# Hybrid decoder step: steps of a packed triangular inverse moved from among the matmul products to places beside the key scores and value products

## The reference

```python
proj = x @ w_in                       # 2048 x 7184
# group A: gated DeltaNet, 8 heads x 128: conv width 4, silu, l2 norms,
#   chunked delta rule over chunks of 128 rows for the prompt:
#   (I + strictly lower part of beta * k k^T * decay)^-1 applied to v and k
# group B: MoBA attention, 8 heads x 128: the prompt's own block;
#   samples score all 2048 cached keys, keep the best 3 blocks of 256,
#   softmax over them and their own key, times the cached values
out = concat(oa, ob) @ w_out;  x = layer_norm(ALPHA * x + out)
x = layer_norm(ALPHA * x + cross_attention(x, 256 memory tokens))
x = layer_norm(ALPHA * x + swiglu(x, w1, w2))   # hidden 5632
```

## Time and profile before

| what | value |
|---|---|
| device time, median of 3 | 1552.3 us (1551.79 to 1552.63) |
| the profiled execution | 1559.02 us |
| its span, first to last instruction | 1557.2 us |
| mean granted TensorE clock | 0.992 |
| busy: PE, DVE, ACT, POOL | 97%, 59%, 42%, 6% |
| DMA moved | 365.11 MB, mean 234 GB/s |
| chain that ended last | PE 79%, DVE 7%, ACT 4%, DMA 4% |

### The profile page before, as it was taken

How to read it: one execution, slowest core, us unless ns; L and a number is a source line. 1 busy time by engine, 2 the same in 40 slices (tenths; PEclk the granted TensorE clock), 3 DMA queues, 4 the chain that set the end, 5 groups by cost and what they waited for, 6 DMA issues and landing times.

```text
span 1557.2 us, 36665 instructions
## 1 busy us (share of the span) xinstructions
PE 1508.7 (97%) x15464; PEld 1458.0 (94%) x15464; DVE 912.4 (59%) x1217; ACT 651.1 (42%) x771; POOL 89.0 (6%) x126
## 2 busy tenths in 40 slices
PE   7999999999889999999999999999999999999996
PEld 7899899999778999997999999999999999999995
DVE  4445646458643466664786666666666644455566
ACT  5344344434425454463643334443333333333344
POOL 0000000002233100001000000000000000000000
PEclk9999999999999999999999999999999999999998
DMA  8788989896678876656555555556767655555453
GB/s 290 262 340 331 338 307 363 304 340 250 248 261 300 311 272 242 217 179 254 190 177 174 171 179 188 169 183 229 251 233 257 208 174 185 189 169 181 162 183 116
DMA packets 72527, 365.11 MB, mean 234 GB/s; under 512 B 9072, under 2 KB 10424, under 8 KB 45656
## 3 DMA queue, kind: packets, MB, share of 16 engines
q1 hardware_dynamic: 56960, 310.00, 56.1%
q0 software_dynamic: 13664, 52.31, 9.1%
q10 hardware_dynamic: 1792, 1.20, 0.3%
HBM read 353.20 MB, written 10.47 MB: 234 GB/s over the span
## 4 chain that ended last, share of the span: by engine, by line
PE 79%; DVE 7%; ACT 4%; DMA 4%; SPq 3%; issue 2%; another core or an unknown queue 1%; POOL 0%; ACTq 0%; DVEq 0%
PE psum_g L538 22%; PE psum_g L539 22%; PE psum_g L540 22%; PE M L2220 3%; DVE wl L522 2%; ACT wh L517 2%; SPq L659 2%; PE M L538 1%; PE M L539 1%; PE M L540 1%; PE psum_g L2560 1%; DMA raw<-w_in_t 1%; DMA sraw<-cache_k_t 1%; PE M L2235 1%
## 5 line engine op out<-in xcount | busy, mean ns | idle before, releaser
L538 PE MATMUL psum_g<-xh,wh 128*128 128x264 f32 (+1 forms) x2382 | 696.5, 292 | 5.9 <-DVE wl L522 3.8
L539 PE MATMUL psum_g<-xl,wh 128*128 128x264 f32 (+1 forms) x2382 | 676.8, 284 | 0.0
L540 PE MATMUL psum_g<-xh,wl 128*128 128x264 f32 (+1 forms) x2382 | 675.9, 284 | 0.0
L522 DVE TENSOR_TENSOR wl<-raw,wh 128x2048 fp32r<-128x2048 f32 (+1 forms) x205 | 461.6, 2252 | 302.4 <-ACT wh L517 301.9
L517 ACT CAST wh<-raw 128x2048 fp32r<-128x2048 f32 (+1 forms) x221 | 414.4, 1875 | 248.2 <-PE psum_g L540 194.4
L538 PEld LDWEIGHTS psum_g<-xh,wh 128*128 128x128 f32 x2382 | 449.4, 189 | 21.7 <-issue 13.3
L539 PEld LDWEIGHTS psum_g<-xl,wh 128*128 128x128 f32 x2382 | 449.8, 189 | 3.2 <-issue 2.9
L540 PEld LDWEIGHTS psum_g<-xh,wl 128*128 128x128 f32 x2382 | 447.9, 188 | 0.0
L538 PE MATMUL psum_g<-gh,wh 128*128 128x264 f32 x704 | 200.3, 285 | 0.2 <-DVE wl L522 0.2
L539 PE MATMUL psum_g<-gl,wh 128*128 128x264 f32 x704 | 199.4, 283 | 0.0
L540 PE MATMUL psum_g<-gh,wl 128*128 128x264 f32 x704 | 199.4, 283 | 0.0
(11 more groups left out here) (474 smaller groups left out, 1693.5 us busy)
## 6 DMA issues: line engine op xcount, KB each, us to landing
raw<-w_t SPq DMA_DIRECT2D x88, 1024.0 KB
raw<-w_in_t SPq DMA_DIRECT2D x53, 1024.0 KB
kring<-cache_k_t SPq DMA_DIRECT2D x96, 512.0 KB, 5.5
sraw<-cache_k_t SPq DMA_DIRECT2D x32, 512.0 KB, 6.5
raw<-w_out_t SPq DMA_DIRECT2D x16, 1024.0 KB
raw<-w2a_t SPq DMA_DIRECT2D x16, 1024.0 KB
raw<-w2b_t SPq DMA_DIRECT2D x16, 1024.0 KB
raw<-w2c_t SPq DMA_DIRECT2D x16, 768.0 KB
```

Source lines behind the costliest of these rows:

```text
L522: eng.tensor_tensor(wl[:, u % 2, 0:nk], raw[:, u % 2, 0:nk], wh[:, u % 2, 0:nk].bitcast(F32), ALU.subtract).then_inc(raw_used, 1)
L538: nc.tensor.matmul(out, hi_w, x_hi(k), start=(k == order[0]), stop=False)
L539: nc.tensor.matmul(out, hi_w, x_lo(k), start=False, stop=False)
L540: last = nc.tensor.matmul(out, lo_w, x_hi(k), start=False, stop=(k == order[-1]))
```

## The change

A table `steps_at(u, place)` says which steps stand at which place. In pairs 0 to 2 steps 7 to 18 stand three a unit at place 3, that is in `behind`: the first ahead of the burst, the second between its halves, the third behind it. In pair 3 they stand two at a time around a group of value products, at place 1 (k = 7) or place 3. Step 19 moves from unit r = 4 to place 0 of r = 5, and `first_chunk` on ScalarE with it. VectorE does all the steps of a place where the place stands in its order; `head_out` comes ahead of `step(1)`. The signal of step 14 on VectorE is split, so that TensorE's step 15 waits for the first of two quarters only.

```diff
-                      [n for l in lv[1:-1] for n in (f"t1_{l}", f"x_{l}", f"y_{l + 1}")] +
+                      [n for l in lv[1:-1] for n in (f"t1_{l}", f"x_{l}") + (("xq",) if l == SMALL - 1 else ()) + (f"y_{l + 1}",)] +
...
+        def steps_at(u, place):
+            p, r = pair_at(u)
+            if p < 0 or r in (0, 7):
+                return (4 * r + place,) if p >= 0 else ()
+            if r == 1 and place < 2:
+                return (4 + place,)
+            if r > 4:
+                return (4 * r + place if (r, place) != (5, 0) else 19,)
+            if p < 3:
+                return tuple(range(3 * r + 4, 3 * r + 7)) if place == 3 else ()
+            if place == 3:
+                return {1: (7, 8), 2: (11, 12), 3: (15, 16)}.get(r, ())
+            return {2: (9, 10), 3: (13, 14), 4: (17, 18)}.get(r, ()) if place == 1 else ()
...
                 elif r == 5:
+                    first_chunk(p)
                     first_state(p)
...
-                if r == 4:
-                    first_chunk(p)
-                elif r == 5:
+                if r == 5:
                     second_chunk(p)
...
                         for q in range(2):
-                            ins = nc.vector.tensor_tensor(quarter(xlo, q), xc[part(q)], small(B_, part(q)), ALU.subtract)
-                        vec(ins)
-                        wait(dve, b_dve, f"x_{l}", p)
+                            vec(nc.vector.tensor_tensor(quarter(xlo, q), xc[part(q)], small(B_, part(q)), ALU.subtract))
+                        wait(dve, b_dve, "xq", p)
...
-                step(1)
                 if 0 <= j - 1 < H:
                     head_out(j - 1)
+                step(1)
...
-            def score(i, u):
+            def score(i, u, heads=range(H)):
...
+            def tiles_at(u, place):
+                steps = steps_at(u, place)
+                return steps if steps and 7 <= steps[0] <= 18 else ()
...
-                if k % 4 == 3 and 0 <= r < 7:
-                    delta(p, 4 * r + k // 4)
+                if k % 4 == 3 and not tiles_at(u, k // 4):
+                    for s in steps_at(u, k // 4):
+                        delta(p, s)
...
+                    first, *rest = tiles_at(u, 1) or (None,)
+                    if first:
+                        delta(p, first)
                     for group in groups_at(u, 0):
                         page_values(group)
+                    for s in rest:
+                        delta(p, s)
...
+                first, *rest = tiles_at(u, 3) or (None,)
+                if first:
+                    delta(p, first)
                 for j in bursts_at(u):
-                    score(j // 4, j % 4)
+                    for half in range(2):
+                        score(j // 4, j % 4, range(4 * half, 4 * half + 4))
+                        if rest:
+                            delta(p, rest.pop(0))
                 if u in (UNITS - 5, UNITS - 4):
                     state_rows(u - (UNITS - 5))
                 for group in groups_at(u, 1):
                     page_values(group)
+                for s in rest:
+                    delta(p, s)
```

More of the change, by code:

```diff
@@ L1724, in _, with step @@
                 j = u - FIRST_HEAD
-                step = lambda c: delta(p, 4 * r + c) if p >= 0 else None
+                def step(place):
+                    for s in steps_at(u, place):
+                        delta(p, s)
                 if 0 <= j - 1 < H:
@@ L2216, in score @@
                     pe.wait_ge(k_full[m % K_RING], 16 * (m // K_RING + 1))
-                for h in range(H):
+                for h in heads:
                     for p, m in enumerate(pages):
```

## The result

| what | before | after |
|---|---|---|
| device time, median | 1553.5 us (1551.79 to 1558.8, 11 runs) | 1571.37 us (1561.01 to 1580.3, 11 runs) |
| the profiled execution | 1559.02 us | 1570.05 us |
| stretches of clock 0.50 in it | 4 | 7 |

The ratio is 1.0106 (95% interval 1.0083 to 1.0128): slower by 1.1%, some 16 us by the ratio and 17.9 by the two medians. The median lies above the range of 1550.5 to 1569.

The account below looks back on a forecast made before the run. TensorE, busy 97% of the span, was taken as the bound, so time between its product groups counts. 1.65 - 0.8 + 3.2 = +4.05 us on the profiled execution, carried over unscaled to 1556.4 us; range 1550.5 to 1569.

Parts of the forecast that it names:

- +1.65 us for pairs 0 to 2: Pairs 0 to 2: each ends 0.55 us late, the stand in unit 14 outweighing savings elsewhere; +1.65 us for three.
- the clock's +3.2 us: TensorE's clock: new stands bring two more falls to half clock than now, +3.2 us; bounds 0 and +9.6.
- -0.8 us for pair 3: Pair 3, beside the value products: six steps leave the products, signals get through, the pair gains 0.8 us.
- The edges: TensorE, half burst to packed step: the change of shape takes 0.21 us; bounds 0.03 and 0.21.
- The cheap change of shape: Faster rival: half burst to packed step takes 0.03 us instead of 0.21; -3.4 us, 1548.9 us; chance 0.14.
- The stand in unit 14: TensorE ahead of step 14, also units 22 and 30: waits 2.5 us for VectorE, busy with convolution and normalising.
- 1.8 us a pair: Pairs 0 to 2: steps placed around bursts save 1.3 us a pair, 1.8 us with the waits.
- head's values 0.35 us late: Pair 3: head turn 1.7 us later because two answers precede the maximum, but the head's values only 0.35 us late.
- The held signals: Slower rival, pair 3: step signals held until 0.8 us after the last gather; +16 us, 1568.8 us; chance 0.26.
- Little happens: Rival: the 0.21 us edge holds but the clock stays up in the stands; +0.9 us, 1553.2 us; chance 0.18.
- three times -0.65 us: Pairs 0 to 2 at the low bound of the change of shape: each pair gains 0.65 us instead of losing.

Follow-up runs that it names:

- two free repeats: The changed kernel, unedited, twice more on one chip, no pair 3 step held: 1566.62 and 1568.19 us, beside 1554.46 for the kernel before.
- x9: Kernel before with new places in pair 3 only, gathers waiting for the step's signal and the scores' maximum ahead of the answers: ratio 0.9951 to the kernel before.
- x14: Changed kernel, with pair 3's gathers waiting for the step's signal and the maximum ahead of the answers: ratio 0.9979 to the kernel before.
- x8: Kernel before with new places in pair 3 only, its gathers waiting for the step's signal: ratio 0.9998 to the kernel before.
- x7: Changed kernel, with pair 3's gathers also waiting for the signal of the step behind the value products: ratio 1.0040 to the kernel before.
- x1: Changed kernel with new places in pairs 0 to 2 only, pair 3 as in the kernel before: ratio 1.0049 to the kernel before.
- x13: Kernel before with new places in pair 3 only and the maximum ahead of the answers, gathers free: ratio 1.0014 to the kernel before.
- x5: Changed kernel with pair 3's scores' maximum ahead of the answers, gathers free: ratio 1.0036 to the kernel before.
- x2: Changed kernel with new places in pair 3 only, pairs 0 to 2 as in the kernel before: ratio 1.0063 to the kernel before.
- r_after: The changed kernel run again unedited (the repeat), its trace with held signals: ratio 1.0075 to the kernel before.
- x12: Changed kernel with gathers waiting, maximum first, and steps 13 to 15 answered ahead of the convolution in pairs 0 to 2: ratio 0.9944 to the kernel before.
- x10: Changed kernel with gathers waiting and steps 13 to 15 answered ahead of the convolution in pairs 0 to 2: ratio 1.0007 to the kernel before.
- x11: Kernel before with new places in pair 3 only, gathers waiting, plus 288 unread small products behind bursts in pairs 0 to 2: ratio 1.0150 to the kernel before.
- x4: Changed kernel plus 16 unread full-size products behind the first half burst of units 14, 22 and 30: ratio 1.0109 to the kernel before.
- x3: Changed kernel with VectorE answering steps 13 to 15 ahead of convolution and normalising in units 14, 22 and 30: ratio 1.0088 to the kernel before.

## Why the prediction was wrong

Two terms of the sum failed: the +1.65 us for pairs 0 to 2 with the clock's +3.2 us, and the -0.8 us for pair 3. In the comparison that the forecast is measured by, the one trace has its signals free, and its loss lies in pairs 0 to 2. In the two free repeats these pairs are 5.5 and 7.2 us longer than in the trace before, of 7.6 and 9.2 us in the whole span. Pair 3 is shown to lose only where its signals are held.

**The edges: right.** 0.20 us measured, 0.21 taken. The cheap change of shape is out.

**+1.65 us for pairs 0 to 2: the step that failed in free executions.** The stand in unit 14 is right in place and size: 2.32, 2.33 and 2.31 us for 2.5, each for VectorE's answer to step 13; none in units 13 and 15. Where nothing else happened, in pair 0 of the first trace, the last step is 0.54 us later than the first is; forecast 0.55. But the sum took the 1.8 us a pair that it saves elsewhere as kept. By the medians pairs 0 to 2 cost 0.28, 0.42 and 0.49% (x9 to x14, x8 to x7, x1), 4.4 to 7.7 us with their falls of the clock; beside a held pair 3 it is less, 0.22 and 0.12% (x13 to x5, x2 to r_after). Forecast were 1.65 us and a share of 3.2. With the stands gone they cost nothing (x9 to x12, x8 to x10) where 1.8 us a pair should have been gained. What is there in its place are the stands for issue, for which the forecast had no term: 2.7 to 4.0 us in the four traces of the kernel after, none in the one before. Twelve steps' matmuls moved next to the bursts' matmuls, and x11 shows that more matmuls there bring such stands. That they are all of the missing gain is argued from these sizes and not shown.

**"-0.8 us for the pair": the step that failed in held executions.** Its pieces are there in the free traces: no signal held, the turn late by 1.9 to 2.3 us, and in the first 103.0 us for the pair against 104.2, -1.2. That is luck as much as working: the free repeats have 101.7 and 104.5 us, and x1's trace, with the old places and its signals held, 101.4. And the old and the new order were not compared under one condition. The earlier trace rows are a held execution, 6.7 us over its median, and the gain was the release of five signals. With held signals in both orders (x1's trace shows them held in the old places in that comparison) the new one costs 0.63% in pair 3 (x2), +10 us with its falls of the clock. The reason is what the forecast saw and took as nearly covered (head's values 0.35 us late): two answers, one of them held, queued ahead of the head's maximum. Taking away the hold brings 0.65% (x8), the queue 0.47% (x9). What the new pair 3 costs against an old one with free signals no trace shows. The two free repeats end 12.2 and 13.7 us behind the kernel before beside them (1554.46), while the trace before was itself at 1559.02; whether that surplus lies in its held signals stays open.

**The clock: the right direction, too small.** The trace has three more stretches at half clock than the earlier trace rows's execution, against two forecast, and its clock of 0.990 is a little above the mean of its runs, 0.988. They reach from 1561.01 us at a mean clock of 0.993 to 1580.3 at 0.984. Beside the kernel before, on one chip, the mean is 0.987 against 0.992 (r_after), an estimate of 8 us for a term of 3.2. The runs don't show it as a cause of its own: it rises as stands go, to 0.989 with the gathers' wait (x7), 0.991 with the convolution later as well (x10), 0.993 with the maximum first too (x12). How much of a stand's price is its length and how much the clock behind it, x4 was to tell and didn't.

**The rivals.** The held signals came in the repeat and in five experiments with free gathers, with the mechanism as written: a signal due 0.15 us after the gather's start, held until past the second or third, maximum and turn behind it. What spoke against it, that these steps are issued ahead of the gathers, does not protect them. It had 0.26. That its 1568.8 us lie near the 1571.37 measured is no proof: the trace of that comparison has its signals free, the comparison with a held one gave 1.0075 only, and how many of the timed runs were held isn't known. The 9 to 12 us of the first comparison's loss that are beyond what pairs 0 to 2 cost by the medians stay open. "Little happens" is out. In the rival of the cheap edge the sum has a slip: three times -0.65 us and 1.65 - 4.3 don't agree (-1.95 and -2.65 us), which with an edge of 0.20 us changes nothing.

## What to carry to other kernels

When instructions are gathered into a block, look first at what the answering engine has queued ahead of and behind its answers: here putting one consumer (the head's maximum) ahead of two answers was worth 0.4 to 0.6%, where the whole change cost 0.75 to 1.06%. Look also at how many matmuls then stand in a row: here the longer rows brought stands for issue. Packed matmuls that signal while GpSimd issues gathers may be answered 2 to 3 us late; let the gathers wait for that signal, and see that the next signal is due after they are through. And take both sides of a comparison from executions in the same condition: if the profiled one is 6.7 us over the median, a gain that consists of removing its disturbances may not be there in the median.

## What the runs showed of the hardware that was not expected

- A packed step's signal issued 0.37 us ahead of the first of three gathers was answered after 3.24 us in one trace of the kernel after and after 0.70 us in another.
- Of TensorE's stands for issue (0.75 to 3.9 us) behind runs of small matmuls, 24 of 24 looked at end 2.3 to 2.6 us after a transfer of queue q8 (instructions), with the DMA engines 97.6% busy (x3) and with 13.4% (x11). 288 more small matmuls made it 16.3 us in all.
- A stand of 2.3 us ahead of step 14 was followed by 1.2 GHz twice in the first trace of the kernel after and not at all in its first free repeat, which has two such stands.
